# S5 input products of a hybrid S5/mLSTM/MoE step: two steps issued together in four 32-row tiles and four PSUM banks

## What is computed

```python
bu_re = jnp.einsum('blgc,gpc->blgp', uf, bbar_re)      # uf: 32 groups of 16 channels; 64 states per group
bu_im = jnp.einsum('blgc,gpc->blgp', uf, bbar_im)
...
y = (jnp.einsum('blgp,gcp->blgc', h_re, c_re.astype(f32))
     - jnp.einsum('blgp,gcp->blgc', h_im, c_im.astype(f32)))
```

## Time and profile before

| | |
|---|---|
| median of 3 runs | 1270.02 us (1268.51 to 1270.38) |
| span of the profiled execution | 1267.5 us |
| PE busy in the span | 1228.0 us (97%) |
| DVE, ACT, POOL busy | 465.3, 174.7, 241.5 us |
| read from HBM | 437.39 MB |

### The profile page before, as it was taken

One profiled execution on the slowest core, in us unless ns is written; L12 is line 12 of the kernel. 1 busy time (PEld: TensorE's weight loads), 2 busy tenths in 40 slices (PEclk: granted clock), 3 DMA queues, 4 the chain that ended last, 5 costly groups with the idle time before them and its releaser, 6 DMA issues.

```text
span 1267.5 us, 21323 instructions
## 1 busy us (share of the span) xinstructions
PE 1228.0 (97%) x7739; PEld 552.1 (44%) x7740; DVE 465.3 (37%) x915; ACT 174.7 (14%) x311; POOL 241.5 (19%) x438
## 2 busy tenths in 40 slices
PE   7999999999899999999999999999999999999997
PEld 5666666668433433333334333333333333333332
DVE  6668757333622322222223222222223222222224
ACT  4651005214400000000000000000000000000002
POOL 2067760000111121111111211111111121111100
PEclk9989999999899999999999999999999999999999
DMA  8323232559699999999999999999999999999994
GB/s 228 100 68 100 93 102 71 158 184 391 241 399 428 428 429 428 428 428 429 429 428 428 428 429 429 428 428 429 429 429 428 428 429 429 430 428 427 429 429 191
DMA packets 69351, 440.29 MB, mean 347 GB/s; under 512 B 13024, under 2 KB 42376, under 8 KB 44744
## 3 DMA queue, kind: packets, MB, share of 16 engines
q1 hardware_dynamic: 66952, 438.72, 84.0%
q10 hardware_dynamic: 2368, 1.15, 0.3%
HBM read 437.39 MB, written 1.87 MB: 347 GB/s over the span
## 4 chain that ended last, share of the span: by engine, by line
PE 69%; DMA 25%; DVE 4%; issue 1%; ACT 0%; DVEq 0%; POOL 0%; SPq 0%; ACTq 0%; POOLq 0%
DMA big<-in_w_gate_up_dram 25%; PE psum L917 23%; PE psum L519 14%; PE psum L960 13%; PE psum L897 5%; PE psum L883 4%; PE psum L497 3%; PE psum L797 3%; PE psum L531 1%; PE psum L628 1%; PE psum L926 1%; PE psum L947 1%; PE psum L639 0%; DVE acc L1842 0%; DVE m L1565 0%
## 5 line engine op out<-in xcount | busy, mean ns | idle before, releaser
L917 PE MATMUL psum<-big,m 128*64 128x512 f32 x2048 | 473.8, 599 | 11.1 <-DMA big<-in_w_gate_up_dram 9.6
L1803 DVE TENSOR_TENSOR acc<-acc,psum 128x512 f32<-128x512 f32 (+1 forms) x192 | 123.1, 681 | 581.4 <-PE psum L897 581.4
L917 PEld LDWEIGHTS psum<-big,m 128*64 128x64 f32 x2048 | 137.5, 137 | 317.9 <-issue 257.9
L960 PE MATMUL psum<-big,m 128*64 128x512 f32 x1024 | 226.8, 595 | 0.0
L519 PE MATMUL psum<-big,m 128*128 128x320 f32 x576 | 166.4, 444 | 2.3 <-issue 1.0
L1359 POOL COPY m<-uT 96x64 bf16 x32 | 7.5, 233 | 660.5 <-PE psum L947 660.2
L519 PEld LDWEIGHTS psum<-big,m 128*128 128x128 f32 x576 | 109.2, 194 | 54.0 <-issue 14.1
L960 PEld LDWEIGHTS psum<-big,m 128*64 128x64 f32 x1024 | 70.7, 137 | 134.1 <-issue 127.9
L897 PE MATMUL psum<-m 64*128 64x512 f32 (+1 forms) x384 | 106.7, 632 | 0.0
L1245 ACT ACTIVATE m<-m 128x512 f32<-128x512 f32 x32 | 20.2, 630 | 559.0 <-DVE m L1816 559.0
L1368 POOL TENSOR_SCALAR m<-cst,m 128x128 f32<-128x128 f32 x96 | 74.8, 789 | 7.7 <-POOL m L1363 7.7
(11 more groups left out here) (283 smaller groups left out, 848.1 us busy)
## 6 DMA issues: line engine op xcount, KB each, us to landing
big<-in_w_gate_up_dram SPq DMA_DIRECT2D x128, 2048.0 KB, 28.6
big<-in_w_down_dram SPq DMA_DIRECT2D x64, 2048.0 KB, 30.6
m<-in_w_in_dram SPq DMA_DIRECT2D x18, 1024.0 KB, 5.2
m<-in_w_s_glu_dram SPq DMA_DIRECT2D x8, 512.0 KB, 4.6
m<-in_w_out_dram SPq DMA_DIRECT2D x3, 1024.0 KB, 5.6
acc<-in_x_prompt_dram SPq DMA_DIRECT2D x4, 512.0 KB, 5.1
m<-in_w_ml_out_dram SPq DMA_DIRECT2D x2, 1024.0 KB, 5.0
big<-in_w_out_dram SPq DMA_DIRECT2D x1, 1024.0 KB, 7.6
```

What stands on the lines that cost most here:

```text
L917: mm = pe.matmul(psum[SLOT * hf:SLOT * hf + SLOT, GB + gu, :], xeT[:, GU_CHUNKS * k + c, :], big[:, base:base + 512], start=(c + k == 0), ...
L960: mm = pe.matmul(psum[SLOT * hf:SLOT * hf + SLOT, DB, :], hT[:, m, c, :], big[:, base:base + 512], start=False, stop=(c == DN_CHUNKS - 1 a ...
L1803: v.tensor_tensor(x, x, psum[0:n, CB + hf, :], ALU.add).then_inc(S("added"), 1)
```

## The change

`s5_in` on PE is issued for two steps at once, in place of every even step: four products in a row, which use all four 32-row tiles, into four banks (2 and 3 for the even step, 5 and 4 for the odd one). The odd step issues nothing. To free banks 4 and 5, S5's outputs and the gate columns go to bank 7, and `natural` uses bank 6 alone. With that, `row_columns` moves from behind slot 9 to behind slot 16, the second part of `natural` from slot 14 to 15, and PE gets further waits.

```diff
+        BU = ((2, 3), (5, 4))
+        YB, RCB = 7, 7
...
-                        (4, "gate_abs"), (4, "softplus"), (5, "state_in"), (6, "gate_scan"), (7, "row_factors"), (9, "row_columns")):
+                        (4, "gate_abs"), (4, "softplus"), (5, "state_in"), (6, "gate_scan"), (7, "row_factors"), (16, "row_columns")):
...
-        for n, j in enumerate((14, 14, 18)):
+        for n, j in enumerate((14, 15, 18)):
...
             def row_columns(_):
 
                 pe.wait_ge(S("rows_ready"), 1)
+                pe.wait_ge(S("y_read"), 1)
...
             def s5_in(j):
 
+                if j % 2 == 1:
+                    return
                 if j == 0:
                     pe.wait_ge(S("setup_read"), SETUP_B)
                     pe.wait_ge(S("u_ready"), 1)
                     pe.wait_ge(S("nmc_ready"), 1)
+                    pe.wait_ge(S("gate_rows"), 1)
                 else:
                     pe.wait_ge(S("bu_read"), j)
                 t = j // 4
-                for k, u in enumerate((uT, uT2)):
-                    s = slice(32 * ((j + 2 * k) % 4), 32 * ((j + 2 * k) % 4) + 32)
-                    mm = pe.matmul(psum[:, 2 + k, 0:T], btz[s, k, t, :], u[s, t, :], start=True, stop=True)
-                mm.then_inc(S("bu_done"), 1)
+                for i in (j, j + 1):
+                    for k, u in enumerate((uT, uT2)):
+                        s = slice(32 * ((i + 2 * k) % 4), 32 * ((i + 2 * k) % 4) + 32)
+                        mm = pe.matmul(psum[:, BU[i % 2][k], 0:T], btz[s, k, t, :], u[s, t, :], start=True, stop=True)
+                mm.then_inc(S("bu_done"), 2)
...
             def s5_out(t):
...
-                if t > 0:
+                if t == 0:
+                    pe.wait_ge(S("dm_read"), 2)
+                else:
                     pe.wait_ge(S("y_read"), t)
+                if t == 1:
+                    pe.wait_ge(S("cols_ready"), 1)
+                if t == 2:
+                    pe.wait_ge(S("st_ready"), 2)
...
             def natural(n):
...
-                if n == 2:
-                    pe.wait_ge(S("nat_read"), 1)
+                else:
+                    pe.wait_ge(S("nat_read"), n)
...
             def scores(a_):
                 if a_ == 0:
                     pe.wait_ge(S("nat_read"), 3)
+                else:
+                    pe.wait_ge(S("y_read"), 2)
...
                 if c == 0:
                     pe.wait_ge(S("st_ready"), 2)
+                    pe.wait_ge(S("y_read"), 4)
```

More of the change, by code:

```diff
@@ L597, in row_columns @@
                             o = (n * NC + c) * 2
-                            pe.matmul(psum[half(hp), 5, o:o + 2], by_chunk(k)[:, c, :], ident[0:H, 2 * hp:2 * hp + 2],
+                            pe.matmul(psum[half(hp), RCB, o:o + 2], by_chunk(k)[:, c, :], ident[0:H, 2 * hp:2 * hp + 2],
                                       start=True, stop=True, skip_group_check=True)
                 for h in range(H):
-                    mm = pe.matmul(psum[:, 5, DEC_AT + h * NC:DEC_AT + (h + 1) * NC], head(h, P), by_chunk(R_WI)[:, :, CH - 1],
+                    mm = pe.matmul(psum[:, RCB, DEC_AT + h * NC:DEC_AT + (h + 1) * NC], head(h, P), by_chunk(R_WI)[:, :, CH - 1],
                                    start=True, stop=True, skip_group_check=True)
@@ L634, in s5_out @@
                 pe.wait_ge(S("setup_read"), SETUP_C)
-                if t > 0:
+                if t == 0:
+                    pe.wait_ge(S("dm_read"), 2)
+                else:
                     pe.wait_ge(S("y_read"), t)
+                if t == 1:
+                    pe.wait_ge(S("cols_ready"), 1)
+                if t == 2:
+                    pe.wait_ge(S("st_ready"), 2)
                 for k in range(2):
                     for q in range(4):
-                        mm = pe.matmul(psum[32 * q:32 * q + 32, 4, 0:T], ctt[:, k, t, 32 * q:32 * q + 32],
+                        mm = pe.matmul(psum[32 * q:32 * q + 32, YB, 0:T], ctt[:, k, t, 32 * q:32 * q + 32],
                                        hh[:, (4 * t + q) % HH, k, :], start=(k == 0), stop=(k == 1), skip_group_check=True)
@@ L652, in natural @@
                         for hp in range(2):
-                            mm = pe.matmul(psum[half(hp), 6 + n % 2, (2 * i + a_) * HD:(2 * i + a_ + 1) * HD],
+                            mm = pe.matmul(psum[half(hp), 6, (2 * i + a_) * HD:(2 * i + a_ + 1) * HD],
                                            kT[:, 2 * hp + a_, c * CH:(c + 1) * CH], ident, start=True, stop=True, skip_group_check=True)
@@ L693, in chunk @@
                 if c == 0:
-                    pe.wait_ge(S("y_read"), 4)
                     pe.wait_ge(S("bu_read"), NJ)
@@ L1071, in row_columns @@
                 act.wait_ge(S("cols_mm"), 1)
-                do(nc.scalar.copy(wcol[:, 0:2], cut(psum[:, 5, 0:2 * NC * 2], 2, NC, 2)))
-                do(nc.scalar.activation(wcol[:, 2], cut(psum[:, 5, 2 * NC * 2:3 * NC * 2], NC, 2), ACT.Exp, scale=-1.0))
-                nc.scalar.copy(flat(dec), psum[:, 5, DEC_AT:DEC_AT + H * NC]).then_inc(S("cols_ready"), 1)
+                do(nc.scalar.copy(wcol[:, 0:2], cut(psum[:, RCB, 0:2 * NC * 2], 2, NC, 2)))
+                do(nc.scalar.activation(wcol[:, 2], cut(psum[:, RCB, 2 * NC * 2:3 * NC * 2], NC, 2), ACT.Exp, scale=-1.0))
+                nc.scalar.copy(flat(dec), psum[:, RCB, DEC_AT:DEC_AT + H * NC]).then_inc(S("cols_ready"), 1)
             def decay_exp(a_):
@@ L1082, in natural @@
                 c1 = min(2 * n + 2, NC)
-                nc.scalar.copy(kn[:, 2 * n:c1], cut(psum[:, 6 + n % 2, 0:(c1 - 2 * n) * 2 * HD], c1 - 2 * n, 2, HD)).then_inc(S("nat_read"), 1)
+                nc.scalar.copy(kn[:, 2 * n:c1], cut(psum[:, 6, 0:(c1 - 2 * n) * 2 * HD], c1 - 2 * n, 2, HD)).then_inc(S("nat_read"), 1)
             def group_root(c):
@@ L1514, in s5_in @@
                 b = j % 2
-                C, Sn, br, bi = ct[:, j, :], sn[:, j, :], psum[:, 2, 0:T], psum[:, 3, 0:T]
+                C, Sn, br, bi = ct[:, j, :], sn[:, j, :], psum[:, BU[b][0], 0:T], psum[:, BU[b][1], 0:T]
                 if j % 4 == 0:
@@ L1539, in s5_out @@
                 dve.wait_ge(S("y_done"), t + 1)
-                do(v.scalar_tensor_tensor(out=uT[:, t, :], in0=uT[:, t, :], scalar=vc[:, 8 + t:9 + t], in1=psum[:, 4, 0:T],
+                do(v.scalar_tensor_tensor(out=uT[:, t, :], in0=uT[:, t, :], scalar=vc[:, 8 + t:9 + t], in1=psum[:, YB, 0:T],
                                           op0=ALU.mult, op1=ALU.add))
```

## The result

The changed kernel takes 1262.82 us (median of 4 runs, 1259.92 to 1263.13) beside 1269.77 us of the kernel before (4 runs): ratio 0.9938, 95% interval 0.9926 to 0.9950. It is faster by 6.95 us; 9.5 us were forecast (1260.5, own range 1259.3 to 1262.1, so the result lies 0.7 us outside of that). The profiled execution took 1262.56 us, with a span of 1260.6 us, 6.9 us under that of before. The page of the changed kernel, PE's busy time and granted clock, answers to the earlier trace rows: the low slice in the S5 stretch is gone, the one at the router is still there.

The account below looks back on a forecast made before the run. PE's instruction stream up to slot 30 was taken as the bound. Terms 6.66 + 3.67 - 0.65 - 0.16 = 9.52 us took 1270.0 to 1260.5 us, own range 1259.3 to 1262.1, whole range 1258.3 to 1267.0.

Parts of the forecast that it names:

- The bound: Up to slot 30 PE's instruction stream sets the end; time removed counts in full within a 3.5 us margin.
- The rival of DVE and POOL as the bound: In the S5 chain, steps of 7.5 us without pause would leave a gain of only 1.2 us; chance 0.07.
- Term 4: Eight calls of four S5 products: each takes 0.75 us against a pair's 0.73, costing 0.16 us in all.
- two pairs: Four tiles run as two pairs one after another, 1.46 us per call, 5.8 us more: 1266.3; chance 0.12.
- single passes: The four tiles' passes run one by one, 3.44 us per call, 21.5 us in all: 1282.0; chance 0.04.
- Term 3: Behind slot 9 PE newly waits for DVE's reads of steps 0 and 1: cost 0.65 us.
- Term 1: Eight odd steps' products leave their places between slots, from step 1 behind slot 8 on: saves 6.66 us.
- other edits, at nothing: `natural` in one bank, moved waits, ACT's columns and SP's weight loads: taken to cost nothing.
- Term 2: Gate columns moved behind slot 16 cost the same there, and the clock's fall near 70 us goes: 3.67 us gained.
- the first rival: The clock falls again behind slot 16 and takes back 3.67 us: 1264.2; chance 0.22.
- The tail: From slot 30 (`s5_out(3)`) to the end all work only moves: distance unchanged at 1076.8 us, within 1 us.

Follow-up runs that it names:

- e5_apart: Changed kernel with its new order and banks, but the odd steps' products issued alone at their own places again: 1270.46 us, ratio 1.0000.
- e2: Kernel before (with a bounded load of the experts' end counts), only `row_columns` moved from behind slot 9 to behind slot 26: 1269.06 us, ratio 1.0004.
- e3: Changed kernel (c_after) with `row_columns` back behind slot 9, ahead of the four products of steps 2 and 3: 1261.89 us, ratio 0.9933.
- c_after: Changed kernel with only PE's load of each expert's end count bounded, the base for the other runs on it: 1261.92 us, ratio 0.9945.
- e7_again: The same program as c_after, measured and profiled a second time: 1264.39 us, ratio 0.9955.
- e8_warm: c_after with twelve unused full products (128 columns) at PE's start, ahead of the first transposes: 1262.69 us, ratio 0.9941.
- e4_twice: c_after with each call of four S5 products issued twice: 1269.23 us, ratio 0.9990.
- e6_fill: c_after with six unused products of 256 columns in PE's three router waits before the experts: 1317.36 us, ratio 1.0365.
- e9_pad6: c_after with six unused products of two columns at PE's start, ahead of the first transposes: 1316.44 us, ratio 1.0369.
- e10_fill18: c_after with both e6_fill's six products in the router waits and e8_warm's twelve at the start: 1262.00 us, ratio 0.9932.

## Why the prediction was right, and where it was off

**The bound** stood. Time taken out before slot 30 went through to the end: the stretch lost 8.77 us and the span 6.9, and the windows of the expert loop didn't change. DVE and POOL ended 3.50 us ahead of PE, the margin forecast (POOL 177.7 forecast, 179.1 measured, of which 0.6 is the later start). That it agrees so closely is in part luck: the sum had DVE working through all steps without pause at 6.76 us each, while it stood idle ahead of four of them, 9.4 us in all, and did five in 4.4 to 5.9 us. The rival of DVE and POOL as the bound didn't happen. The warning of the Trainium skill that reading out may become the bottleneck (TensorEngine Tiling (Array Packing), PSUM Bottleneck) isn't borne out here: PE waits for DVE's reads once, 0.67 us, and did so for 0.68 before.

**Term 4** was right: 0.75 us per call. The rivals of two pairs and of single passes are out; e5_apart gives the pair 0.74. The Trainium skill (TensorE: Matmul & The Clock Gate, Measured speedup vs the span model) has a factor of 3.07 for four row tiles, from which the prediction made an estimate of 0.95 per call. That doesn't show in these fp32 products of 320 columns: four together take 0.75 us, two together 0.74. The Trainium skill gives that factor for 512 columns and names no data type beside it; the bf16 is the prediction's.

**Term 3** was right: 0.65 forecast, 0.67 measured.

**Term 1**, 6.66, was nearly right. (The pair between slots 12 and 13 in the earlier trace rows is step 4's; step 5's stands between 13 and 14, as the term has it.) From slot 8 to slot 10's start PE takes 10.30 us, where the terms add up to 10.43. Slots 13 and 14 gave 0.90 for 0.88, slots 21 and 27 0.60 and 0.56 for 0.59. What failed in it is "only the pair goes: 4 x 0.73": behind slots 11 and 19 only 0.58 and 0.47 went, as PE's wait for its own products became longer (0.30 and 0.41). That is 0.41 us. `natural`, which "other edits, at nothing" passed over, costs 0.16 for being split.

**Term 2** is the step that failed, in mechanism and in size. "It costs the same behind slot 16" is off by 0.51 us: before, the columns ran beside the next pair. And "I take 3.67, by the nearest row" took one profile's fall for a property of the order. In the profile of after the fall is indeed gone, and slot 10 gave 2.34 for 2.28. But e2 moved the columns alone to such a place and gained nothing in the median, e3 put them back and lost nothing, and the first rival's fall behind slot 16 is there in three of seven profiles with the same S5 order. In the medians term 2 is worth about nothing or little. Its exact share isn't settled: the four runs of e3 lie 1.2 us above the lower group of the changed kernel and 2.6 below the upper one, and a 3 us effect that comes and goes between executions is as large as what the runs tell apart.

**The tail.** "If it differs by over 1 us, my claim ... is wrong": it differs by 1.2 us. The work behind slot 30 only moved, but how long the clock stays low at expert 0 did not. The tails of six profiles of the changed S5 order without fillers (after, c_after, e3_cols9, e7_again, e8_warm, e4_twice) go from 1076.3 to 1078.4.

So 9.5 was forecast and 6.95 found. In the profiles the difference is 0.51 + 0.41 + 0.16 = 1.1 us of sized terms (0.75 net in the stretch, since other places gave a few tenths more), and 0.7 + 1.2 of start-up and tail. That the medians (6.95) and the two profiled spans (6.9) differ by nearly the same is luck, since start-up and tail vary by 1 to 2 us between profiles. The forecast counted a gain of the clock in full that the executions hold at most in part. And the result is no support for term 2: the whole range went up to 1267.0 and held the time without it too, 1264.2.

## What to carry to other kernels

Here small products on row tiles that don't share rows or banks cost by the call and not by the tile (two tiles 0.74 us, four 0.75): fill the array in one call, and let the steps between wide products become fewer. Before a fall of the clock is booked as the price of what stands ahead of it, move that alone and look at several profiles and at all runs, not at the median only. And if a kernel grows by tens of us after an edit far from the place that lost them, compare the instruction queue's packets on the two pages first.

## What the runs showed of the hardware beyond that

- Number of products ahead of a loop: 6 more products of PE ahead of the loop over the experts cost 54 us (e6_fill, e9_pad6: 84 instruction packets, 1.38 MB), while 12, 18 and 32 more cost nothing (e8_warm, e10_fill18, e4_twice: 21 packets, 0.34 MB). The 64 packets more go with 14 waits of PE of up to 4.6 us, two each time that the loop starts anew, beside a DMA share of 1.01. Why it happens, and for which numbers of products, stays open.
- In three of seven profiles with the changed kernel's S5 order the clock falls to the low level for some 3.4 us behind each of two groups of few-row products of 2.8 to 2.9 us, in the four others behind neither, and each such fall costs 1.7 us. The seven are not all one program: they differ in products elsewhere.
- A second set of four 32-row products right behind the first costs 0.54 us, the first one 0.75.
- Products of four rows and of 32 rows run at the same time (67.28 to 67.61 in e3_cols9).
